# The first stage of a transformer kernel: modulation rows transposed in pairs and summed by VectorE, four chunks and then five products

## The reference

```python
def _modulation(cvec, w, b):
    m = jax.nn.silu(cvec) @ w + b          # w: 2048 x 6144
    return shift, scale, gate              # three parts of 2048

shift, scale, gate = _modulation(c, mod_w, mod_b)
shift_c, scale_c, gate_c = _modulation(c_ctx, mod_w, mod_b)
h  = _rmsnorm(x, pre_g)   * (1 + scale)   + shift      # 512 tokens
hc = _rmsnorm(ctx, pre_g) * (1 + scale_c) + shift_c    # 256 tokens
proj = h @ w_in                                        # q, k, v, z
kv_ctx = hc @ w_in[:, Q_W:Q_W + KV_W]
```

## Time and profile before

| | |
|---|---|
| median of three runs | 2729.41 us (2726.91 to 2730.3) |
| the profiled execution | 2724.89 us |
| its span (first to last instruction) | 2722.8 us |
| TensorE busy | 2603.7 us (96%) |
| DVE busy | 1703.4 us (63%) |
| ACT busy | 949.9 us (35%) |
| TensorE's mean clock | 0.977 of full |
| read from HBM | 371.85 MB, 143 GB/s over the span |
| the first stage | up to about 161 us |

### The profile page before, as it was taken

How to read it: one execution, slowest core, us unless ns; L and a number is a source line. 1 busy time by engine, 2 the same in 40 slices (tenths; PEclk the granted TensorE clock), 3 DMA queues, 4 the chain that set the end, 5 groups by cost and what they waited for, 6 DMA issues and landing times.

```text
span 2722.8 us, 32062 instructions
## 1 busy us (share of the span) xinstructions
PE 2603.7 (96%) x12787; PEld 2097.3 (77%) x12787; DVE 1703.4 (63%) x2824; ACT 949.9 (35%) x1510; POOL 132.4 (5%) x121
## 2 busy tenths in 40 slices
PE   7999999999988999999998998999999999999898
PEld 5789676677766887888777887877878878878686
DVE  4445766767775868777777877667465444445422
ACT  3222343343343333332323333344354422223221
POOL 0000000000000103000010112000000000000000
PEclk7999999999999998999999997999999999999999
DMA  9935332333334653656647553444222223322432
GB/s 349 333 130 169 124 106 96 115 117 124 124 108 150 206 170 128 205 181 194 189 153 244 191 178 135 139 141 150 74 78 85 82 82 90 99 82 82 151 116 70
DMA packets 358566, 390.72 MB, mean 143 GB/s; under 512 B 11842, under 2 KB 352450, under 8 KB 354578
## 3 DMA queue, kind: packets, MB, share of 16 engines
q1 hardware_dynamic: 352144, 354.79, 41.0%
q0 software_dynamic: 6128, 33.89, 3.3%
q10 hardware_dynamic: 146, 0.00, 0.0%
HBM read 371.85 MB, written 16.78 MB: 143 GB/s over the span
## 4 chain that ended last, share of the span: by engine, by line
PE 79%; DVE 11%; issue 3%; DMA 3%; ACT 3%; SPq 1%; POOL 0%; DVEq 0%; ACTq 0%; POOLq 0%
PE G L1762 65%; PE OB L1762 5%; PE S L1762 5%; DVE MACC L1320 3%; PE TB L1762 3%; DVE WLO L1314 1%; PE TB L1765 1%; DVE TT L1314 1%; DMA MRAW<-in_w_ada 1%; ACT WHI L1006 1%; DMA MORE<-in_ev_mod_w 1%; DMA LATE<-in_ev_mod_w 1%; DVE Y L1314 1%; SPq L877 1%; DVE SM L1498 1%
## 5 line engine op out<-in xcount | busy, mean ns | idle before, releaser
L1762 PE MATMUL G<-HHI,WHI 128*128 128x512 f32 x2624 | 1109.6, 423 | 43.8 <-issue 20.4
L1762 PE MATMUL G<-HHI,WLO 128*128 128x512 f32 x2624 | 1032.7, 394 | 0.0
L1762 PE MATMUL G<-HLO,WHI 128*128 128x512 f32 x2624 | 1030.8, 393 | 0.0
L1314 DVE TENSOR_TENSOR WLO<-RAW,WHI 128x1024 fp32r<-128x1024 f32 x376 | 461.5, 1230 | 264.8 <-ACT WHI L1006 261.8
L1762 PEld LDWEIGHTS G<-HHI,WHI 128*128 128x128 f32 x2624 | 498.2, 190 | 167.4 <-issue 50.1
L1006 ACT ACTIVATE WHI<-RAW 128x1024 fp32r<-128x1024 f32 x376 | 395.0, 1053 | 586.8 <-PE G L1762 548.6
L1762 PEld LDWEIGHTS G<-HLO,WHI 128*128 128x128 f32 x2624 | 498.6, 190 | 114.1 <-issue 18.9
L1762 PEld LDWEIGHTS G<-HHI,WLO 128*128 128x128 f32 x2624 | 496.9, 189 | 110.3
L1320 DVE SCALAR_TENSOR_TENSOR MACC<-MRAW,SC,MACC 128x256 f32<-128x256 f32 x840 | 435.6, 519 | 91.0 <-DMA MRAW<-in_od_mod_w 35.7
L1762 PE MATMUL G<-WHI,HHI 128*128 128x256 f32 x640 | 186.3, 291 | 0.0
L1762 PE MATMUL G<-WLO,HHI 128*128 128x256 f32 x640 | 181.0, 283 | 0.0
(11 more groups left out here) (262 smaller groups left out, 2399.1 us busy)
## 6 DMA issues: line engine op xcount, KB each, us to landing
RAW<-in_w_in SPq DMA_DIRECT2D x128, 512.0 KB, 3.8
MRAW<-in_od_mod_w SPq DMA_DIRECT2D x96, 512.0 KB, 4.8
MRAW<-in_w_ada SPq DMA_DIRECT2D x96, 512.0 KB, 5.1
RAW<-in_ev_w_in SPq DMA_DIRECT2D x80, 512.0 KB, 3.8
RAW<-in_od_w_in SPq DMA_DIRECT2D x64, 512.0 KB, 4.1
MRAW<-in_ev_mod_w SPq DMA_DIRECT2D x54, 512.0 KB, 5.0
RAW<-in_ev_w_out SPq DMA_DIRECT2D x32, 512.0 KB, 3.5
RAW<-in_od_w_out SPq DMA_DIRECT2D x32, 512.0 KB, 3.5
```

Source lines behind the costliest of these rows:

```text
L1314: return e.o.tensor_tensor(o, a, b, op)
L1762: return e.o.matmul(o, l, r, start=start, stop=stop, skip_group_check=True)
```

## The change

In the first stage, the turn of a row into columns is done for two rows at once. Four transposes (one for each 128 columns of the two rows in ROW) put them into TB, 128x512, and one DVE reduction adds the four positions of c and of c_ctx into a small tile CB; bias and pre_g are added as before. The table t_r4 and its load are gone. The tile RB is gone too: `x_cast` transposes each column of factors read as a broadcast.

The plan is laid out anew. All four chunks of a row stand together, then come up to five pieces. The columns of a pair stand, for rows up to 7, behind the last chunk of the pair's second row; from row 10 on one row later. The pieces of pair 0 may run from chunk 9 on. The blocks of w_in are requested behind chunk 0 (two) and 4 (one), and split behind 6, between columns and tiles of pair 0, and behind 12.

```diff
-                if i in (1, 3, 5):
+                for _ in range({0: 2, 4: 1}.get(i, 0)):
                     load_next()
                 if c == 3:
                     put("row_copy", n)
                 if i == 3:
                     put("x_cast")
-                if i in (9, 11, 13):
+                if i in (6, 12):
                     split_next()
-                if c == 1 and n > 0:
-                    put("row_cols", n - 1)
+                if i > 51 and i % 4 == 3:
+                    put("x_spill", i // 4 - 13, i)
+                if c == 3 and (n % 2 if n < 8 else n > 8 and n % 2 == 0):
+                    m = n // 2 if n < 8 else n // 2 - 1
+                    put("pair_cols", m)
+                    if i == 7:
+                        split_next()
+                    put("h_pair", m)
+                    near, lent = pieces(m), near
+                    ready += lent
+                elif i == 9 or c == 3:
                     ready += near
                     near = []
-                    if n % 2 == 0:
-                        put("h_pair", n // 2 - 1)
-                        near = pieces(n // 2 - 1)
-                if i > 51 and i % 4 == 3:
-                    put("x_spill", i // 4 - 13, i)
-                for _ in range((0, 2, 0, 3)[i % 4]):
-                    if ready:
-                        kv_piece(*ready.pop(0))
-            put("row_cols", len(order0) - 1)
+                if i == 9 or c == 3:
+                    for _ in range(5):
+                        if ready:
+                            kv_piece(*ready.pop(0))
+            put("pair_cols", 7)
             put("h_pair", 7)
```

On ACT, the copy of row n >= 2 now waits for the columns of pair n//2-1. On DVE:

```diff
-                e.wait_ge(v_rs, ("in", 4))
                 e.wait_ge(v_intro, "sc")
                 e.o.tensor_copy(NORM2, RS[:, 2:6]).then_inc(*v_rs.up(("in", "kept")))
-                for n in range(6):
-                    ts(RB[:, n, :], ONE[:, :], RS[:, 24 + n:25 + n], None, MUL).then_inc(*v_xn.up(n))
...
+            elif stage == "pair_cols":
+                i, = a
+                e.wait_ge(p_cols, i)
+                if i:
+                    e.wait_ge(v_cols, (i - 1, "end"))
+                e.o.tensor_reduce(CB[:, :, :], TB[:, :].rearrange("p (g j r) -> p g r j", g=4, j=4)[:, :, 0:2, :], AX_X,
+                                  ADD).then_inc(*v_cols.up((i, "sums")))
+                e.wait_ge(v_cols, (i, "sums"))
+                for n, nb in enumerate((i, 8 + i)):
+                    bias = COL[:, 160 + 2 * nb:162 + 2 * nb]
+                    for v, t in enumerate((MOD[:, 0, 2 * nb:2 * nb + 2], MODX[:, 2 * nb:2 * nb + 2])):
+                        tt(t, CB[:, 2 * n:2 * n + 2, v], bias, ADD).then_inc(*v_cols.up((i, n, v)))
+                for v, t in enumerate((MOD[:, 0, 16 + 2 * i:18 + 2 * i], MODX[:, 16 + 2 * i:18 + 2 * i])):
+                    e.wait_ge(v_cols, (i, 1, v))
+                    stt(t, t, 1.0, COL[:, 48 + 2 * i:50 + 2 * i], ADD, MUL).then_inc(*v_cols.up((i, "end")))
```

And on TensorE:

```diff
-                    tr(OB[:, n * P:(n + 1) * P], RB[:, n, :])
+                    tr(OB[:, n * P:(n + 1) * P], RS[:, 24 + n:25 + n].to_broadcast([P, P]))
...
-            elif stage == "row_cols":
-                n, = a
-                e.wait_ge(a_row, n)
+            elif stage == "pair_cols":
+                i, = a
+                e.wait_ge(a_row, 2 * i + 1)
                 e.wait_ge(*tb)
-                for nt in range(2):
-                    t = mm(TB[:, 2 * nt:2 * nt + 2], ROW[n % 2][:, nt * P:(nt + 1) * P], SM[:, 40:42],
-                           nt == 0, nt == 1)
-                t.then_inc(*p_cols.up(n))
-                tb = v_cols, (n, "end")
+                for g in range(4):
+                    t = tr(TB[:, g * P:(g + 1) * P], ROW[g // 2][:, g % 2 * P:(g % 2 + 1) * P])
+                t.then_inc(*p_cols.up(i))
+                tb = v_cols, (i, "sums")
```

More of the change, by code:

```diff
@@ L31 @@
          [("b_ada_2", 0, 48)]]
-TABLES = ["t_sq", "t_mask", "t_sb", "t_r4", "t_rope_a", "t_rope_b", "t_rcnt", "t_decay"]
+TABLES = ["t_sq", "t_mask", "t_sb", "t_rope_a", "t_rope_b", "t_rcnt", "t_decay"]
 class Sig:
@@ L116, in build @@
     DUMP, _ = place("DUMP", [P, D], F32, d0)
-    RB, _ = place("RB", [P, 6, P], F32, d0 - 2048)
     IDN, _ = place("IDN", [P, P], F32)
@@ L147, in build @@
     RS = scratch("RS", [P, 32], F32, 44 * K1)
+    CB = scratch("CB", [P, 4, 2], F32, 44 * K1 + 128)
     SC32 = scratch("SC32", [P, KT, 32], F32, 42 * K1)
@@ L204, in build @@
     a_ph, a_st, a_out, a_sum = on_chip("a_ph", "a_st", "a_out", "a_sum")
-    v_intro, v_wlo, v_xt, v_rs, v_xn, v_cols, v_h, v_acc, v_mod, v_nr, v_sm, v_gate, v_silu = on_chip(
-        "v_intro", "v_wlo", "v_xt", "v_rs", "v_xn", "v_cols", "v_h", "v_acc", "v_mod", "v_nr", "v_sm", "v_gate",
+    v_intro, v_wlo, v_xt, v_rs, v_cols, v_h, v_acc, v_mod, v_nr, v_sm, v_gate, v_silu = on_chip(
+        "v_intro", "v_wlo", "v_xt", "v_rs", "v_cols", "v_h", "v_acc", "v_mod", "v_nr", "v_sm", "v_gate",
         "v_silu")
@@ L1024, in act_program @@
         e.o.dma_start(SM[0:1, 0:8], T["ev_sink"]).then_inc(*sel.up("sink", by=16))
-        e.o.dma_start(SM[:, 40:42], T["t_r4"]).then_inc(*sel.up("r4", by=16))
         e.o.add_instruction(mybir.InstLoadActFuncSet(
@@ L1064, in act_program @@
                 if n >= 2:
-                    e.wait_ge(p_cols, n - 2)
+                    e.wait_ge(p_cols, n // 2 - 1)
                 cp(ROW[n % 2][:, :], S[:, 512:768]).then_inc(*a_row.up(n))
@@ L1373, in dve_program @@
                 e.o.tensor_copy(TY[:, :], TB[:, :]).then_inc(*v_xt.up("cast"))
-            elif stage == "row_cols":
-                n, = a
[L1376 to L1386, removed]
+            elif stage == "pair_cols":
[13 more added lines that the diff above has]
+                    stt(t, t, 1.0, COL[:, 48 + 2 * i:50 + 2 * i], ADD, MUL).then_inc(*v_cols.up((i, "end")))
             elif stage == "h_pair":
                 i, = a
-                e.wait_ge(v_cols, (2 * i + 1, "end"))
+                e.wait_ge(v_cols, (i, "end"))
                 e.wait_ge(v_xt, "cast")
@@ L1779, in pe_program @@
         e.wait_ge(par, "par")
-        e.wait_ge(sel, "r4")
+        e.wait_ge(sel, "sink")
         for i in range(3):
@@ L1801, in pe_program @@
             elif stage == "x_cast":
-                e.wait_ge(v_xn, 5)
+                e.wait_ge(v_rs, ("in", 4))
                 e.wait_ge(*tb)
@@ L1805, in pe_program @@
                 for n in range(2):
-                    tr(OB[:, n * P:(n + 1) * P], RB[:, n, :])
+                    tr(OB[:, n * P:(n + 1) * P], RS[:, 24 + n:25 + n].to_broadcast([P, P]))
                 for n in range(2, 6):
-                    t = tr(TB[:, (n - 2) * P:(n - 1) * P], RB[:, n, :])
+                    t = tr(TB[:, (n - 2) * P:(n - 1) * P], RS[:, 24 + n:25 + n].to_broadcast([P, P]))
                 t.then_inc(*p_xt.up("cast"))
@@ L2161, in tables @@
     dec = np.where(rel[None] >= 0, np.exp(np.maximum(rel, 0)[None] * g[:, None, None]), 0.0) * SCALE
-    r4 = np.stack([i % 32 == 0, i % 32 == 1], axis=1).astype(f4)
-    return {"t_r4": r4, "t_sq": sq, "t_mask": mask, "t_sb": sb, "t_rope_a": rope(ang.astype(np.float64)),
+    return {"t_sq": sq, "t_mask": mask, "t_sb": sb, "t_rope_a": rope(ang.astype(np.float64)),
             "t_rope_b": rope(ang2.astype(np.float64)), "t_rcnt": rc, "t_decay": dec.astype(f4)}
```

## The result

The median of the changed kernel is 2731.48 us (20 runs, 2720.81 to 2736.97), that of the kernel before 2726.76 us over 20 runs. The ratio is 1.0016, 95% interval 1.0008 to 1.0023: 4.4 us slower, 2 to 6 us (the two medians differ by 4.7). The three runs of before that were at hand for the prediction lay 2.7 us above this longer median, so part of the closeness of 2729.9 to 2731.5 is luck: the forecast said 0.5 us later, and 4.4 was measured. The profiled execution of the changed kernel has a span of 2729.8 us, 7.0 above before.

A forecast was written before the change was run, and what follows sets the result against it. TensorE (7.08 us a row) bound the stage, close to the loads (6.75). 1.9 us gained by row 13 were given back in the tail: stage 0.5 us later, 2729.4+0.5 = 2729.9 us, range 2721 to 2738.

The forecast's parts named there:

- (1) Columns: Four transposes for a pair cost 0.44 us instead of 0.94, 0.25 less a row; odd rows' hand-over some 0.7.
- the 2.6 that I let show: Eight rows from 68 to 125 us: at most 0.33 us a row can show, 2.6 us in all.
- (2) Four chunks, five products: Each row: fewer switches save about 0.2 us; with cheaper columns TensorE needs 6.65 us, under the loads' 6.75.
- (3) Order of pairs: Early stage: ten products fill TensorE's idle time, the first near 45.7 us; 0 us lost (0 to 3).
- the moved block: Ten products run early: up to 4.5 us of TensorE work out of the way, worth nothing where the queue binds.
- The tail: Rows 13 to 15: four buffers refilled in one burst, spills 3 us each; last chunk done at 143.1 us.
- The rival on the clock: Waits bring half clock at rows 11 to 13 and in the tail: 5.4 us on top, 2735.3 us; chance 0.20.
- (5) The reduction: DVE's part of a pair: reduction 0.2 us, chain 0.4 longer, counted once; hole before the last pair about 0.6.
- After the last chunk: End of the stage: products, columns and hole take 18.6 us against 15.9 before; the stage ends at 161.7.
- Everything behind it moves unchanged: Rest of the program behind the first stage: TensorE's queue, moved unchanged, giving a span of 2723.3 us.
- fewer holes: Bursts cost nothing and the spill comes behind the last load: stage ends at 156.2, 2724.4 us; chance 0.20.
- TensorE's saving counts whole: First stage: loads can come faster than 1.50 us a chunk, so 8.4 us are gained, 2721.0 us; chance 0.12.

The follow-up runs named there:

- method: The kernel before with its old plan, only the columns made the new way (four transposes and one reduction per pair): stage end 155.4 us, ratio 0.9978.
- cover: The changed kernel without products behind chunk 9, so pair 0's second five lie behind row 3: stage end 164.0 us, ratio to before 1.0008.
- tail: The changed kernel with two products behind the second chunk and three behind the fourth from row 12 on: stage end 166.4 us, ratio to before 1.0010.
- after_spill: The changed kernel with the first two spills moved behind chunk 63: stage end 164.7 us, ratio to before 0.9999.
- m_spill: Against method, the first two spills moved behind chunk 63: stage end 153.6 us, ratio to before 0.9959.

## Why the prediction was right or wrong, point by point

**Sign and size.** Within 0.2% held the highest chance and happened; slightly slower was said and was measured. The size, 0.5 us for the whole, was missed by 4, and for the stage (161.7 forecast, 171.5 measured) by 10; the total is nearer than its parts because some 4 us were given back behind the stage, which no step had.

**(1) Columns.** The prediction counts eight matmul records a row for the old way; the earlier trace rows has four (x4), and the 0.47 us that it worked with stands. Four transposes took 0.36 us in the last pair (157.52 to 157.88), 0.44 was said. The hand-over in odd rows is a wait of 0.50 us for ACT three times, with the transposes 0.9 to 1.1, where 1.1 was said. The gain came through where the old order was kept: in method 1.9 us by row 13, within the 2.6 that I let show, and 3.8 more in the last two rows, where the clock stayed at 1.00 while both profiles of before have 6.8 us at half. That the earlier arrival kept the clock up is argued, not shown: no run held the one fixed and moved the other.

**(2) Four chunks, five products.** Rows 5 and 6 of the changed kernel take 71.79 to 85.40, 13.6 us or 6.8 a row with the hand-over; 6.65 was said without it. Right in size. The loads at 1.50 us held too: in row 12 the chunks came at 119.47, 120.98 and 122.49. That the queue would be the limit throughout was wrong for the change from 60 to 100 (335 and 297 GB/s) and right for it around rows 11 and 12, and for method (349, 347, 340).

**(3) Order of pairs: the step that failed.** The first product came at 46.15 (45.7 said), and rows 3 and 4 were done at 59.7 and 62.7 (59.7 follows from the working, 62.8 with the hand-over). But I wrote that the moved block was "worth nothing where the queue binds" and that rows 3 and 10 have none, without asking what stands between the columns and the first product of pair 1. I had written down this very chain, 4.1 us from tiles to product, for pair 0 and for pair 7, and not used it for pair 1. Cost: 3.1 us of wait and 1.5 of low clock at once, 4.5 by row 5 (73.7 against 69.2 in the working); 6.8 to 7.5 at the stage's end by the run cover, against the three profiles of the change. The prediction's list of what is queued behind named the wait for ACT, not this one.

**The tail.** For the ends of rows 13, 14 and 15 I had 123.5, 134.1 and 143.1; measured 132.6, 144.3 and 153.2. The steps between are 10.6 and 9.0 against 11.8 and 8.9: near in size. What was off is the start. Row 12 was already 6.9 us late (123.6 against 116.6), from the early hole and what it drags; five products at half clock added 2.2. The working let j56 go out just when the queue ran empty; with those products in front the queue stood nearly still for some 5 us. And the parts of the burst were not what the sum took: tail and after_spill put the refill at 0.6 to 3.1 us in these rows, and the spills at 2, plus the clock, instead of 3 each. That the steps still fit is in part luck. The rival on the clock had it right that such waits bring half clock at rows 11 to 13 and in the tail, with 5.4 us for both; it charged them on top of the sum, where they came with the late products. The first profile has two stretches of 6.8 us there, from 121.7 and from 142.2.

**(5) The reduction.** 0.2 us was taken; it took 0.19, and from reduction to tiles 0.83 us, 0.37 more than the earlier trace rows. The hole in front of the last pair was said at 0.6 and was 0.68.

```profile
158.16 0.19 DVE L1380 TENSOR_REDUCE CB<-TB 128x8 f32<-128x32 f32 x1 [4.39 <-PE TB L1768]
...
158.99 0.75 DVE L1324 SCALAR_TENSOR_TENSOR SQ<-XR,MOD,TY 128x512 f32<-128x512 f32 x1
```

**After the last chunk** 18.6 was said; 153.2 to 171.65 is 18.4.

**Everything behind it moves unchanged.** Not quite: about 4 us less, of which 0.8 to 1.7 have a place; the rest is open.

**The rivals.** The stage end of fewer holes (156.2) was reached only by the old order, method and m_spill with 155.4 and 153.6; with the bursts the holes came. That TensorE's saving counts whole did not happen: the loads stayed at 1.50 us a chunk wherever nothing else moved.

## What to carry to other kernels

When a plan moves filler work earlier, ask at each place from which it was taken what chain it covered; a block of products was worth nothing as work there, and 4.5 us as cover. Where a few buffers are reloaded on use, the spacing of the uses is the spacing of the loads: in the changed kernel, using all four in one visit left the queue all but empty while the engine was busy, and the engine idle while the queue filled. It also puts more of the engine's other work behind the last load, 2.1 us here. And a change made of several edits should be taken apart: here one edit was worth 6 us, and the reordering that came with it cost 16 in the stage (155.4 against 171.5). Of these the experiments place 9.8; the other 6.3 lie in the rest of the plan, and only the waits for tiles are seen in them.

## What the runs showed of the hardware that was not expected

The cost of a wait of TensorE is not its length. In the changed kernel a wait of 3.1 us, and later a row of waits of 0.8 to 0.9, went with stretches at half clock in which five products took 5.95 and 6.4 us instead of 4.4; but the same wait of 3.08 us was followed by none in tail, and so was a single wait of 1.6 us in method. A second profile of the same kernel puts the first stage's end within 0.7 us, though the stretches themselves lie elsewhere, while behind the stage the same program differs by steps of 1 to 2.4 us. And of two writes of 1 MB to memory, a third of the tail's bytes, only the first shows a cost, about 2 us in the row behind it in either order of work; with the bursts, a lower clock came on top.
